# A hybrid decoder layer on one core: the last down projection in token layout, and the gate projection in fp32 column groups

## The reference, cut to what matters

```python
def swiglu(x, w1, w3, w2):
    return (jax.nn.silu(x @ w1) * (x @ w3)) @ w2

x = x + 0.5 * swiglu(rms_norm(x, ffn1_norm), ffn1_w1, ffn1_w3, ffn1_w2)     # D_FF = 2816
h = rms_norm(x, mix_norm)
proj = h @ w_in                                  # columns of all head groups
gq, gk, gv, gr, ga, aq, ak, av = jnp.split(proj, offsets, axis=-1)          # ga: 16 columns
log_a = jax.nn.log_sigmoid(ga @ gla_w_a2 + gla_b_a) / GLA_TAU
...                                              # gated linear attention, dilated attention
x = x + jnp.concatenate([o_gla, o_att], axis=-1) @ w_out
x = x + 0.5 * swiglu(rms_norm(x, ffn2_norm), ffn2_w1, ffn2_w3, ffn2_w2)
return rms_norm(x, final_norm)
```

## Time and profile before

| | us |
|---|---|
| runs shown (3) | 1006.94, 1007.03, 1011.97 |
| median | 1007.03 |
| profiled execution | 1006.93 |
| its span | 1005.1 |
| TensorE busy (PE) | 977.9 (97%) |
| VectorE busy (DVE) | 474.7 (47%) |
| ScalarE busy (ACT) | 336.4 (33%) |
| DMA, mean | 92 GB/s, 92.35 MB |

### The profile page before, as it was taken

The page is one execution under the profiler, slowest core; times in us unless marked ns, Lnnn a source line. Parts: engine busy times, 40 slices in busy tenths (PEclk is TensorE's granted clock), DMA queues, the critical chain, the costliest instruction groups (busy, mean ns, idle before and its releaser), DMA issues.

```text
span 1005.1 us, 11939 instructions
## 1 busy us (share of the span) xinstructions
PE 977.9 (97%) x4568; PEld 803.3 (80%) x4568; DVE 474.7 (47%) x577; ACT 336.4 (33%) x448; POOL 50.8 (5%) x35
## 2 busy tenths in 40 slices
PE   8999999999999999999989999999999999999995
PEld 6788888888888887888767777888888888888884
DVE  6844532244543455744375436654453334344343
ACT  7323222222322344422455554433332122232320
POOL 0950000000000000000121000000000000000000
PEclk9999999999999999999999999999999999999997
DMA  8232222332221333222211103223212232322222
GB/s 299 87 123 83 75 93 95 115 116 93 83 91 56 104 104 126 84 84 85 84 42 43 43 1 118 93 84 116 92 63 94 95 125 90 119 83 69 67 73 83
DMA packets 16479, 92.35 MB, mean 92 GB/s; under 512 B 1968, under 2 KB 2112, under 8 KB 8896
## 3 DMA queue, kind: packets, MB, share of 16 engines
q1 hardware_dynamic: 15728, 90.86, 26.0%
q10 hardware_dynamic: 720, 1.07, 0.3%
HBM read 89.82 MB, written 2.10 MB: 91 GB/s over the span
## 4 chain that ended last, share of the span: by engine, by line
PE 91%; DVE 4%; ACT 2%; issue 1%; DMA 1%; SPq 1%; POOL 0%; DVEq 0%; ACTq 0%; POOLq 0%
PE bank L1007 29%; PE bank L1008 29%; PE bank L1009 29%; PE bank L1280 1%; DMA raw<-in_up 1%; PE bank L1250 1%; ACT w_hi L386 1%; DVE w_lo L632 1%; PE bank L1264 1%; DVE probs L803 0%; DVE sumsq L731 0%; DVE x L999 0%; PE bank L1178 0%; PE bank L1319 0%; PE bank L1184 0%
## 5 line engine op out<-in xcount | busy, mean ns | idle before, releaser
L1007 PE MATMUL bank<-h_hi,w_hi 128*128 128x512 f32 x848 | 333.8, 394 | 2.6 <-DVE gate L672 1.4
L1009 PE MATMUL bank<-h_hi,w_lo 128*128 128x512 f32 x848 | 331.4, 391 | 0.0
L1008 PE MATMUL bank<-h_lo,w_hi 128*128 128x512 f32 x848 | 331.4, 391 | 0.0
L386 ACT ACTIVATE w_hi<-raw 128x2048 fp32r<-128x2048 f32 (+2 forms) x92 | 158.2, 1719 | 328.8 <-PE bank L1009 328.1
L632 DVE TENSOR_TENSOR w_lo<-raw,w_hi 128x2048 fp32r<-128x2048 f32 (+2 forms) x92 | 188.9, 2053 | 70.6 <-ACT w_hi L386 70.4
L1007 PEld LDWEIGHTS bank<-h_hi,w_hi 128*128 128x128 f32 x848 | 160.0, 189 | 39.5 <-issue 2.3
L1009 PEld LDWEIGHTS bank<-h_hi,w_lo 128*128 128x128 f32 x848 | 159.9, 189 | 33.4
L1008 PEld LDWEIGHTS bank<-h_lo,w_hi 128*128 128x128 f32 x848 | 159.9, 189 | 33.3 <-issue 0.5
L1007 PE MATMUL bank<-g_hi,w_hi 128*128 128x512 f32 x352 | 136.9, 389 | 0.0
L1008 PE MATMUL bank<-g_lo,w_hi 128*128 128x512 f32 x352 | 136.9, 389 | 0.0
L1009 PE MATMUL bank<-g_hi,w_lo 128*128 128x512 f32 x352 | 136.9, 389 | 0.0
(11 more groups left out here) (195 smaller groups left out, 690.8 us busy)
## 6 DMA issues: line engine op xcount, KB each, us to landing
raw<-in_up SPq DMA_DIRECT2D x43, 1024.0 KB, 4.8
raw<-in_w_proj SPq DMA_DIRECT2D x8, 1024.0 KB, 4.8
raw<-in_down1a SPq DMA_DIRECT2D x8, 768.0 KB, 4.3
raw<-in_down2a SPq DMA_DIRECT2D x8, 768.0 KB, 4.2
raw<-in_down1b SPq DMA_DIRECT2D x8, 640.0 KB, 3.8
raw<-in_down2b SPq DMA_DIRECT2D x8, 640.0 KB, 3.9
raw<-in_w_v SPq DMA_DIRECT2D x4, 1024.0 KB, 4.9
raw<-in_w_o SPq DMA_DIRECT2D x4, 1024.0 KB, 4.7
```

Source lines behind the costliest of these rows:

```text
L386: nc.scalar.activation(w_hi[u % 2][:, 0:size], raw[u % 2][:, 0:size], ACT.Copy).then_inc(w_round, 1)
L1007: nc.tensor.matmul(out, a_hi, b_hi, start=first, stop=False)
L1008: nc.tensor.matmul(out, a_hi, b_lo, start=False, stop=False)
L1009: return nc.tensor.matmul(out, a_lo, b_hi, start=False, stop=last)
```

## The change

**Gate projection.** The gate weight (16 columns, padded to 32) leaves the weight units; it is loaded at the start into `raw_ga`, VectorE multiplies it by the mixer's gain, and 8 fp32 matmuls multiply it with `x` itself: chunk k goes to column group k % 4 of the array, that is to partitions 32(k % 4) and on of the bank, so that four partial results stand above each other. The low-rank weight `wa2` is repeated four times over the partitions, and its matmul adds them up. The order on TensorE becomes: first query tile, gate, sums, second query tile, low-rank matmuls. All later units have a number that is one lower.

**x to tokens.** In the second up phase of FFN 2 TensorE turns `x` (final but for the last down phase) into four token tiles, 32 transposes of 128x128, after the first and the second unit; ScalarE copies them into `x_tok`.

**Last down phase.** For 128 tokens and 512 output channels at a time, with 128x128 blocks of `g_hi` and `g_lo` as the stationary operand and the weights moving. All 8 banks hold an output tile (4 token tiles x 2 halves). Chunks 0 to 6 are done chunk by chunk over all eight, chunks 7 to 9 (`STAIR = 3`) tile by tile.

**The end.** Per token tile: add to `x_tok`, square with accumulation along the row (ScalarE), mean, root, refinement, multiplication with root and a gain row in one operation, store. For the last token tile the gain is multiplied first, and the two halves are scaled on VectorE and ScalarE.

```diff
-MIX_UNITS = 1 + 4 + 2 + 2 + 4 + 4
+MIX_UNITS = 4 + 2 + 2 + 4 + 4
+GA_COLS = 32
+LAST_KC = PARTS[1][1] - PARTS[1][0]
+LAST_UNITS, STAIR = LAST_KC // 2, 3
...
+        U_LAST = 2 * FFN_UNITS + MIX_UNITS - KC
+        T_LAST = 2 * FFN_TILES + MIX_TILES - KC
+        def last_bank(t, half):
+            return ps[(4 + 2 * t + half) % 8]
...
# SP
                     sp.dma_start(pos_i[:], positions.partition_broadcast(P)).then_inc(pos_landed, 16)
+                    sp.dma_start(raw_ga[:].rearrange("p k c -> p (k c)"), w_ga).then_inc(ga_in, 16)
...
+                    elif u0 == U_LAST:
+                        for v in range(LAST_UNITS):
+                            load(u0 + v, 0, down[1][v])
+                            if v == 0:
+                                sp.dma_start(gain_row[:], final_gain.partition_broadcast(P)).then_inc(gain_landed, 16)
...
-            for m in range(0, KC, 2):
-                sp.wait_ge(fin_done, m + 1)
-                sp.dma_start(outT[m], x[:, m, :]).then_inc(stored, 16)
+            for n in range(2 * ST - 1):
+                t, cols = n // 2, slice(n % 2 * S, n % 2 * S + S)
+                sp.wait_ge(fin_done, n + 1)
+                sp.dma_start(out[t][:, cols], x_tok[:, t, cols]).then_inc(stored, 16)
...
# ScalarE
+            def move_x(t):
+                for half in range(2):
+                    act.wait_ge(x_turned, 2 * t + half + 1)
+                    nc.scalar.activation(x_tok[:, t, half * S:half * S + S], ps[4 + 2 * (t % 2) + half][:],
+                                         ACT.Copy).then_inc(x_moved, 1)
...
+                        up(0, 0, u0 == 0)
+                        if turned:
+                            move_x(0)
+                            move_x(1)
                         up(0, 1)
+                        if turned:
+                            move_x(2)
+                            move_x(3)
...
+            nc.scalar.activation(credit[:], credit[:], ACT.Sqrt)
+            for v in range(2, LAST_UNITS):
+                act.wait_ge(unit_done, v - 1)
+                split(U_LAST + v, 0, UP_W)
+            junk = (square, sumsq)
+            for t in range(ST):
+                for half in range(2):
+                    n = 2 * t + half
+                    act.wait_ge(tok_added, n + 1)
+                    if n >= 2:
+                        act.wait_ge(tok_squared, n - 1)
+                    nc.scalar.activation(junk[half][:], x_tok[:, t, half * S:half * S + S], ACT.Square,
+                                         accum_out=tok_sq[:, n:n + 1]).then_inc(tok_squared, 1)
+                act.wait_ge(tok_mean, t + 1)
+                nc.scalar.activation(nrm[:, 1, t:t + 1], tok_ms[:, t:t + 1], ACT.Sqrt,
+                                     bias=const[:, C_EPS:C_EPS + 1]).then_inc(tok_root, 1)
+            act.wait_ge(tok_rstd, ST)
+            act.wait_ge(tok_weighed, 2)
+            nc.scalar.activation(x_tok[:, ST - 1, S:D], ffn_mem[2][2][:], ACT.Copy,
+                                 scale=nrm[:, 1, ST - 1:ST]).then_inc(fin_last, 1)
+            act.wait_ge(fin_last, 1)
+            act.dma_start(out[ST - 1][:, S:D], x_tok[:, ST - 1, S:D]).then_inc(stored, 16)
...
# VectorE
+            dve.wait_ge(ga_in, 16)
+            nc.vector.tensor_tensor(w_gate[:], raw_ga[:], gains[:, G_MIX:G_MIX + KC, :].broadcast_to([P, KC, GA_COLS]),
+                                    ALU.mult).then_inc(ga_scaled, 1)
             mean_square(1, ps[6][:], D, rstd[:])
...
+            query_tile(0, T)
+            dve.wait_ge(tile_done, T + 2)
             nc.vector.tensor_tensor(projT[:, T_GA, :], ps[4][:], rstd[:], ALU.mult).then_inc(tile_out, 1)
-            split_next(U, 0)
...
+            def token_norm(spare):
+                for t in range(ST):
+                    for half in range(2):
+                        cols = slice(half * S, half * S + S)
+                        dve.wait_ge(tile_done, T_LAST + 2 * t + half + 1)
+                        nc.vector.scalar_tensor_tensor(x_tok[:, t, cols], last_bank(t, half)[:], 0.5, x_tok[:, t, cols],
+                                                       ALU.mult, ALU.add).then_inc(tok_added, 1)
+                        if t == ST - 1:
+                            dve.wait_ge(tok_added, 2 * t + half + 1)
+                            nc.vector.tensor_tensor(spare[half][:], x_tok[:, t, cols], gain_row[:, cols],
+                                                    ALU.mult).then_inc(tok_weighed, 1)
+                    one = slice(t, t + 1)
+                    dve.wait_ge(tok_squared, 2 * t + 2)
+                    nc.vector.tensor_scalar(tok_ms[:, one], tok_sq[:, 2 * t:2 * t + 1], tok_sq[:, 2 * t + 1:2 * t + 2],
+                                            1.0 / D, ALU.add, ALU.mult).then_inc(tok_mean, 1)
+                    ...
+                    refined_root(one).then_inc(tok_rstd, 1)
+                    dve.wait_ge(tok_rstd, t + 1)
+                    if t < ST - 1:
+                        for half in range(2):
+                            cols = slice(half * S, half * S + S)
+                            nc.vector.scalar_tensor_tensor(x_tok[:, t, cols], x_tok[:, t, cols], nrm[:, 1, one],
+                                                           gain_row[:, cols], ALU.mult, ALU.mult).then_inc(fin_done, 1)
+                dve.wait_ge(tok_weighed, 2)
+                nc.vector.tensor_scalar(x_tok[:, ST - 1, 0:S], spare[0][:], nrm[:, 1, ST - 1:ST], None,
+                                        ALU.mult).then_inc(fin_done, 1)
...
# TensorE
+            def turn_x(t):
+                for half in range(2):
+                    if t >= 2:
+                        pe.wait_ge(x_moved, 2 * (t - 2) + half + 1)
+                    for c in range(4):
+                        last = nc.tensor.transpose(ps[4 + 2 * (t % 2) + half][:, c * P:(c + 1) * P],
+                                                   x[:, 4 * half + c, t * P:(t + 1) * P], ident)
+                    last.then_inc(x_turned, 1)
...
+                        step(0, 0)
+                        pe.wait_ge(tile_out, BANK_CREDIT + t0)
+                        turn_x(0)
+                        turn_x(1)
+                        step(0, 1)
+                        turn_x(2)
+                        turn_x(3)
...
-            tile_of(U_MIX % 2, 0, 4, wait=h_ready, base=8)
+            tile_of(U_MIX % 2, 0, 0, wait=h_ready, base=8)
+            pe.wait_ge(ga_scaled, 1)
+            for k in range(KC):
+                g = k % 4
+                last = nc.tensor.matmul(ps[4][GA_COLS * g:GA_COLS * (g + 1), :], w_gate[:, k, :], x[:, k, :],
+                                        start=k < 4, stop=k >= 4)
+            last.then_inc(tile_done, 1)
             pe.wait_ge(sq_added, 9)
             channel_sums(1, 6, sumsq[:])
...
+            tile_of(U_MIX % 2, 1, 1)
...
+            def last_product(t, half, k):
+                tok, slot, col = slice(t * P, (t + 1) * P), (U_LAST + k // 2) % 2, k % 2 * D + half * S
+                return product(last_bank(t, half)[:], g_hi[:, k, tok], g_lo[:, k, tok], w_hi[slot][:, col:col + S],
+                               w_lo[slot][:, col:col + S], k == 0, k == LAST_KC - 1)
+            pe.wait_ge(x_moved, 2 * ST)
+            for k in range(LAST_KC - STAIR):
+                ...
+                for t in range(ST):
+                    if k == 0 and t >= 2:
+                        pe.wait_ge(tile_out, BANK_CREDIT + T_LAST - 2 * (3 - t))
+                    for half in range(2):
+                        ins = last_product(t, half, k)
+                if k % 2:
+                    ins.then_inc(unit_done, 1)
+            pe.wait_ge(w_split, U_LAST + LAST_UNITS)
+            pe.wait_ge(g_ready, 2 * FT)
+            for t in range(ST):
+                for half in range(2):
+                    for k in range(LAST_KC - STAIR, LAST_KC):
+                        ins = last_product(t, half, k)
+                    ins.then_inc(tile_done, 1)
```

More of the change, by code:

```diff
@@ L164, in layer_program @@
         att_g = [sb(f"att_g{g}", [P, S], F32, late) for g in range(GLA_H)]
+        raw_ga = sb("raw_ga", [P, KC, GA_COLS], F32, late)
+        w_gate = sb("w_gate", [P, KC, GA_COLS], F32, late)
         late.close()
@@ L272, in layer_program, with in_tokens @@
         T_MIX, T_FFN2 = FFN_TILES, FFN_TILES + MIX_TILES
-        N_UNITS = 2 * FFN_UNITS + MIX_UNITS
+        U_LAST = 2 * FFN_UNITS + MIX_UNITS - KC
+        N_UNITS = U_LAST + LAST_UNITS
+        T_LAST = 2 * FFN_TILES + MIX_TILES - KC
+        def last_bank(t, half):
+            return ps[(4 + 2 * t + half) % 8]
+        def in_tokens(layer, kind, a):
+            return layer == 2 and kind == "down" and a > 0
         def ffn_phases(u0, t0):
@@ L692, in down @@
                                 low_h(8 + m, m, next_gain)
-                            if not (layer == 2 and isinstance(i, int) and m == KC - 1):
-                                add_square(layer + 1, m)
```

(35 more changed lines are left out.)

120 lines of the change are left out of this document (68 added, 52 removed).

## The result

| | before | changed |
|---|---|---|
| first measurement, median (range), us | 1009.32 (1006.94 to 1011.97), 6 runs | 1001.67 (999.86 to 1003.25), 6 runs |
| ratio, 95% interval | | 0.9926 [0.9905, 0.9946] |
| again, in more rounds, us | 1007.07 (11 runs) | 1001.83 (7 runs) |
| ratio, 95% interval | | 0.9935 [0.9910, 0.9959] |
| profiled execution, us | 1006.93 | 999.86 |

A forecast was written before the change was run, and what follows sets the result against it. TensorE, busy for 97% of the span, was taken as the bound. Gate -1.7, turning x +4.2 and end -6.2 summed to -3.7 us: span 1001.4, time 1003.2 us, range 1000.9 to 1008.3.

The forecast's parts named there:

- Gate: Gate projection in column groups, with one query tile moved ahead of the sums: -1.7 us in all.
- Stall: Before the gate matmuls, TensorE waits 1.35 us for VectorE's product of gain and weight.
- second stall: Before the low-rank matmuls, TensorE waits 0.2 us for the gate's evacuation.
- allowance of 0.4 us: In the eight gate matmuls, 0.4 us for entering and leaving tiled mode, added to 1.7 for 2.1 us.
- Weight loads: At the gate, skill rule that loads overlap running matmuls only across differing row groups; said to speak against the edit.
- the rival of 0.15: At the gate, the stall and narrow sums bring the clock down: +1.7 us, 1004.9 us; chance 0.15.
- Turning x: In the second up phase, 32 transposes of x in two blocks, all on the path: +4.2 us.
- Last phase: Last down phase, 80 products of 3 matmuls before and after: 0 us, no hole.
- fifth weight unit: In the last down phase, the tightest weight unit, split with 1.2 us to spare.
- The end: After the last matmul, 9.6 us instead of 15.8 with VectorE falling behind per token tile: -6.2 us.
- the line at 1002: For the whole kernel, a time under 1002 us counts as faster, 0.5% (5 us) being distinguishable from no change.
- 0.21 for faster: Chance of a time under 1002 us, from the shorter-end rival and the forecast's lower edge.

The follow-up runs named there:

- e3: Changed kernel with all eight gate matmuls in one column group instead of four; profiled span 1007.4 us, 1002.3 without clock drops.
- e8: Changed kernel with four last-phase chunks tile by tile instead of three, fifth weight unit awaited only at its first chunk; one run, 1007.94 us.
- e4: Changed kernel with each transpose of x done four times in place, 96 more; profiled span 1013.4 us, 1006.6 without clock drops.
- e7: Changed kernel with two last-phase chunks tile by tile instead of three; profiled span 1005.5 us, 1000.4 without clock drops.
- e5: Changed kernel again, unedited, in more rounds; 1001.83 us against 1007.07 before, ratio 0.9935.
- e6: Changed kernel with gate weight scaled earlier on VectorE and each token tile's weighing moved into the next tile's wait for squares; 1000.16 us, ratio to before 0.9910.
- e9: e6 without the last norm's three root refinement steps; 999.49 us against 1008.95 before, ratio 0.9910.
- e1: Kernel before with only the gate projection in column groups and its new order; 1005.76 us against 1007.16 before, ratio 0.9980.

## Why the prediction came out as it did

**Gate.** Right in every step, each a little too dear. Stall 1.25 us (1.35), gate 1.86 (2.1), second stall 0.17, which is 0.08 more than before had there (0.2). From the start of the low-rank matmuls to the second matmul of the next tile it was 2.05 us, and 2.25 before; the forecast had no such term. Together 2.3 to 2.5 us instead of 1.7. The allowance of 0.4 us for going in and out of the tiled mode, taken from L1165, was mostly not paid. The overlap was read rightly from a row that mixed rows and columns; e3 shows it for columns alone. The Trainium skill's 2.38x for three column groups (TensorE: Matmul & The Clock Gate, Part 3) would have given an estimated 2.9 us, 1.0 us too much.

**Weight loads.** The prediction let the Trainium skill's rule that weight loads overlap running matmuls only where the row group differs (TensorE: Matmul & The Clock Gate, Part 3) speak against the edit. This case's traces do not bear it out, and the earlier trace rows already did not: in 54.6 us without a hole, by matmuls that use every row, weight loads were busy for 44.87 us.

**Clock at the gate.** It did not fall there in any of the ten traces with this order, eight of them with a stall of about 1.25 us. That a wait of TensorE can bring the clock down, as the rival of 0.15 had it, e8 shows in a wait of 2.97 us.

**Turning x.** 3.5 us instead of 4.2. The 0.119 us came from a row whose 1.9 us hold the drain of the last transpose as well; e4 gives 0.109 each, 3.5 for 32, and the two block entries cost next to nothing.

**Last phase.** No change, no hole: as forecast. The fifth weight unit was split at 971.10 and needed near 972.3, 1.2 us spare as forecast.

**The end.** 9.5 us against 9.6 forecast. The queue on VectorE was the whole point: round 4.85 us (forecast 4.9), and e7 and e8 move the end to 13.5 and 6.6 us by changing only how fast the tiles come. This was not luck: counted as in the forecast, from the end of the second half of token tile 0, VectorE is through with tiles 0 to 2 at 4.3, 9.1 and 14.0 us (forecast 4.3, 9.2, 14.1) and the last result is there at 18.9 (19.2). Only the store took 2.85 us instead of 2.6, which made up for most of that.

**The sum.** Two terms were mis-sized, the turning (4.2, measured 3.5) and the gate (-1.7, measured -2.4), both the same way: -3.7 forecast, -5.2 without drops, and 1.7 us more in the profiled pair, from one drop less. The median of 1001.67 is what the change alone gives from the forecast's base: 1006.93 is a run with two drops, 1006.9 - 5.2 is 1001.7, and the profiled run of e5, with two drops, took 1001.83. So the forecast's 1.5 us too much are these two terms. The 7.6 us between the medians are more than 5.2 because before's median stood at 1009.32 in that measurement, 2.4 us above its profiled run. The time, 1001.67, lies in the range, but on the far side of the line at 1002: most of the chance (0.74) stood on "within 0.5%", and it was faster by 0.65 to 0.74%. The change itself, 5.2 of 1005 us, is 0.52%, just on that line; drops did the rest. With a forecast 1.2 us from that line, 0.21 for faster was too little.

**What was missed.** The spread of the runs was taken for noise of 5 us. In the profiled runs it is the number of clock drops in and behind the attention stage, one to four of 1.7 us (and two more at e8's wait): without them the two traces of the changed kernel agree within 0.2 us (996.4 and 996.6). The times of the other runs fall near steps of 1.7 us too, for before near 1005.5, 1007, 1008.5, 1010 and 1012.

## What to carry to other kernels

Where an engine works through tiles at the end of a kernel, compare its round per tile with the rate at which tiles come: if the round is longer, the backlog grows with every tile, and filling its waits with the work of the tile before pays (1.3 us off the end in e6), about as much as a shorter chain in every tile (1.2 us in e9). But look at what the moved work then stands in front of: in e6 the last tile's mean waited 1.2 us behind it. Small matmuls in separate column groups run side by side at fp32, in both orders tried, but the operand that they need must not be queued behind a split. Before timing differences of a few us, count the drops of the granted clock in each trace and compare the spans without them.

## What the runs showed of the hardware

- A drop of the granted clock held for 3.4 us and cost 1.7 us of dense work, near 507, 520, 545, 562 and 607 us, where waits and thin matmuls alternate. In e1 at 562 and in e8 at 975 two followed directly upon one another. How many a run has changed from run to run of one kernel (one and two in the two traces of the changed kernel).
- Transposes alone kept TensorE at the 2.4 GHz level for 7.15 us (e4, twice).
- Eight fp32 matmuls of 32 columns took 1.86 us in four column groups and 7.0 in one, a factor of 3.75. All groups shared their rows. The order of the groups made no difference (1.86 and 1.87 us), nor did that a group's four instructions stood one behind the other.
- Dependent operations of VectorE on one column follow each other at 0.2 us, the reciprocal as well as the products (978.50, 978.70, 978.90, 979.09 in the changed kernel's last norm).
